# Prompt attention of a hybrid decoder step: the second head's division moved to GpSimd

## The reference, cut to what matters

```python
s = q @ k.T / 8 + bias + log(count)     # 1024 x 1024, causal
e = exp(s - max(s));  p = e / sum(e)
att = p @ v                              # 1024 x 64 for each head
merged = concat(rms_norm(att, g_out_att), rms_norm(y_conv, g_out_conv))
h = h + merged @ w_out
```

## Time and profile before

| | us |
|---|---|
| median of 3 runs | 1403.39 (1402.79 to 1406.4) |
| profiled execution, its own time | 1402.83 |
| its span, first to last instruction | 1401.0 |
| first score matmul of the stage (L1697) starts | 402.1 |
| last matmul of P V (L1724) starts | 551.6 |

### The profile page before, as it was taken

One profiled execution on the slowest core, in us unless ns is written; L12 is line 12 of the kernel. 1 busy time (PEld: TensorE's weight loads), 2 busy tenths in 40 slices (PEclk: granted clock), 3 DMA queues, 4 the chain that ended last, 5 costly groups with the idle time before them and its releaser, 6 DMA issues.

```text
span 1401.0 us, 13600 instructions
## 1 busy us (share of the span) xinstructions
PE 1215.4 (87%) x4994; PEld 651.9 (47%) x4994; DVE 431.5 (31%) x972; ACT 326.2 (23%) x637; POOL 169.5 (12%) x171
## 2 busy tenths in 40 slices
PE   4999999999978887866999938888889898789995
PEld 1444445666645555732455524444344434334442
DVE  1121212221147777311255581411111111033332
ACT  2132322000027664411011110111111111133332
POOL 0001000000030113000001131121212221000000
PEclk9999999999979998877999958999999999979998
DMA  8011400111050102879612054788888888522200
GB/s 271 36 45 60 124 15 19 45 41 64 0 159 31 31 2 62 236 217 325 247 61 72 37 199 140 274 302 354 299 340 300 340 306 344 223 93 98 92 29 34
DMA packets 63660, 209.15 MB, mean 149 GB/s; under 512 B 15198, under 2 KB 28926, under 8 KB 47728
## 3 DMA queue, kind: packets, MB, share of 16 engines
q1 hardware_dynamic: 50560, 177.64, 36.3%
q0 software_dynamic: 13040, 30.71, 5.7%
HBM read 191.81 MB, written 27.52 MB: 157 GB/s over the span
## 4 chain that ended last, share of the span: by engine, by line
PE 71%; DMA 12%; DVE 8%; issue 4%; ACT 3%; POOL 1%; SPq 1%; POOLq 0%; DVEq 0%; ACTq 0%
PE pair L1618 12%; PE pair L1670 12%; PE pair L1939 9%; PE pair L1855 8%; PE pair L2042 8%; DMA R<-m_dram,lists 7%; PE pair L1962 4%; DMA R<-in_cache_v 3%; PE pair L1697 3%; PE pair L1711 2%; PE pair L2024 2%; PE pair L1724 2%; DVE R L1455 2%; DVE R L1229 1%; PE pair L1748 1%
## 5 line engine op out<-in xcount | busy, mean ns | idle before, releaser
L1939 PE MATMUL pair<-R 128*128 128x512 f32 (+1 forms) x512 | 201.3, 617 | 19.9 <-DVE R L1455 19.9
L1670 PE MATMUL pair<-R 128*128 128x352 f32 x576 | 172.5, 463 | 0.4 <-ACT kts L868 0.4
L1618 PE MATMUL pair<-R 128*128 128x512 f32 x384 | 170.2, 601 | 0.8 <-DVE R L1121 0.8
L1670 PEld LDWEIGHTS pair<-R 128*128 128x128 f32 x576 | 110.2, 192 | 61.8 <-issue 1.5
L1939 PEld LDWEIGHTS pair<-R 128*128 128x128 f32 (+1 forms) x512 | 79.6, 180 | 124.8 <-issue 99.1
L1855 PE MATMUL pair<-R 128*128 128x512 f32 x256 | 115.5, 606 | 0.0
L2042 PE MATMUL pair<-R 128*128 128x512 f32 x256 | 114.2, 605 | 0.8 <-ACT R L1053 0.8
L1618 PEld LDWEIGHTS pair<-R 128*128 128x128 f32 x384 | 72.9, 193 | 87.5 <-issue 86.3
L1962 PE MATMUL pair<-R,bias_s 128*128 128x512 f32 (+1 forms) x256 | 98.0, 597 | 0.7 <-ACT bias_s L1009 0.7
L2042 PEld LDWEIGHTS pair<-R 128*128 128x128 f32 x256 | 49.7, 194 | 63.7 <-issue 63.7
L1460 DVE TENSOR_TENSOR R<-pair,R 128x256 f32<-128x256 f32 x27 | 11.5, 425 | 206.6 <-ACT R L1005 206.5
(11 more groups left out here) (280 smaller groups left out, 1280.9 us busy)
## 6 DMA issues: line engine op xcount, KB each, us to landing
R<-in_w_gate SPq DMA_DIRECT2D x32, 1024.0 KB, 8.3
R<-in_w_up SPq DMA_DIRECT2D x32, 1024.0 KB, 11.1
R<-in_w_down SPq DMA_DIRECT2D x32, 1024.0 KB, 5.0
R<-in_x_prompt SPq DMA_DIRECT2D x16, 512.0 KB, 3.4
R<-in_cache_k SPq DMA_DIRECT2D x8, 1024.0 KB, 9.1
R<-in_cache_v SPq DMA_DIRECT2D x8, 1024.0 KB, 18.6
R<-y_dram SPq DMA_DIRECT2D x16, 512.0 KB, 4.3
R<-in_w_in SPq DMA_DIRECT2D x3, 2048.0 KB, 14.9
```

Of the source, the lines that this page charges most:

```text
L1618: last = mm(bk[4 + part][0:n, :], xTs[a.u][:, c, 0:n], wA[:, c, AD * part:AD * part + AD], start=(c == 0), stop=(c == DC - 1))
L1670: last = mm(bk[b][:, 0:n], wB[q % 2][:, c, which, :], xT[:, c, lo:lo + n], start=(c == 0), stop=(c == DC - 1))
L1939: last = mm(bk[2 + u][r, :].rearrange("p (w f) -> p w f", w=2), xgT[u][:, c, r], wgu[s][:, :, c, :], start=(c == 0), stop=(c == DC - 1))
```

## The change

The second head's product moves from DVE's list to Pool's; DVE keeps its reciprocal. `p_ready` becomes two semaphores, one for each head. The squares, the addition and the gain of a pair move from one block behind the pair to single operations behind Pool's division of three successive steps: the squares of pair 0, 1 and 2 stand behind steps 11, 19 and 27, the addition (pairs 1 and 2) behind steps 20 and 28, the gain behind steps 13, 21 and 29. Those of the last pair stand at the end, as before. No other list changes.

```diff
-        for pair in range(NG):
+        def normalise(n, hh):
+            w = P * (STEPS[n][1] + 1)
+            k = 2 * (n % 2) + hh
+            pool.wait_ge(S("rden"), 2 * n + hh + 1)
+            pool.tensor_scalar(E[n % 2][hh][:, 0:w], E[n % 2][hh][:, 0:w], rden[:, k:k + 1], None, ALU.mult).then_inc(S("p_ready1"), 1)
+
+        def squares(pair):
             pool.wait_ge(S("ot_free"), 8 * (pair + 1))
             rows = aT[:, pair, 0:SEQ]
-            if pair >= 1:
-                pool.wait_ge(S("a_sum"), pair)
             if pair == 0:
                 pool.tensor_tensor(a_sum, rows, rows, ALU.mult).then_inc(S("a_sum"), 1)
             else:
                 pool.tensor_tensor(a_sq, rows, rows, ALU.mult).then_inc(S("a_sq"), 1)
...
+        for n in range(NSTEP):
+            normalise(n, 1)
+            pair, k = (n - 3) // 8 - 1, (n - 3) % 8
+            if pair >= 0 and k == 0:
+                squares(pair)
+            if pair >= 1 and k == 1:
+                add_squares(pair)
+            if pair >= 0 and k == 2:
+                scale_a(pair)
+        squares(NG - 1)
+        add_squares(NG - 1)
+        scale_a(NG - 1)
...
+        def invert(n, hh):
+            k = 2 * (n % 2) + hh
+            dve.wait_ge(S("exp_done"), 2 * n + hh + 1)
+            dve.reciprocal(rden[:, k:k + 1], den[:, k:k + 1]).then_inc(S("rden"), 1)
...
             normalise(n, 0)
-            normalise(n, 1)
+            invert(n, 1)
...
-                pe.wait_ge(S("p_ready"), 2 * n + hh + 1)
+                pe.wait_ge(S(f"p_ready{hh}"), n + 1)
```

More of the change, by code:

```diff
@@ L706, in _, with add_squares, scale_a @@
                 pool.tensor_tensor(a_sq, rows, rows, ALU.mult).then_inc(S("a_sq"), 1)
-                pool.wait_ge(S("a_sq"), pair)
-                pool.tensor_tensor(a_sum, a_sum, a_sq, ALU.add).then_inc(S("a_sum"), 1)
-                pool.wait_ge(S("a_sum"), pair + 1)
-            pool.tensor_scalar(rows, rows, gatt[:, pair:pair + 1], None, ALU.mult).then_inc(S("a_scaled"), 1)
+        def add_squares(pair):
+            pool.wait_ge(S("a_sum"), pair)
+            pool.wait_ge(S("a_sq"), pair)
+            pool.tensor_tensor(a_sum, a_sum, a_sq, ALU.add).then_inc(S("a_sum"), 1)
+        def scale_a(pair):
+            rows = aT[:, pair, 0:SEQ]
+            pool.wait_ge(S("a_sum"), pair + 1)
+            pool.tensor_scalar(rows, rows, gatt[:, pair:pair + 1], None, ALU.mult).then_inc(S("a_scaled"), 1)
+        for n in range(NSTEP):
[10 more added lines that the diff above has]
+        scale_a(NG - 1)
         def store_m(a):
@@ L1225, in normalise @@
             k = 2 * (n % 2) + hh
-            dve.wait_ge(S("exp_done"), 2 * n + hh + 1)
-            dve.reciprocal(rden[:, k:k + 1], den[:, k:k + 1]).then_inc(S("rden"), 1)
+            invert(n, hh)
             dve.wait_ge(S("rden"), 2 * n + hh + 1)
-            dve.tensor_scalar(E[n % 2][hh][:, 0:w], E[n % 2][hh][:, 0:w], rden[:, k:k + 1], None, ALU.mult).then_inc(S("p_ready"), 1)
+            dve.tensor_scalar(E[n % 2][hh][:, 0:w], E[n % 2][hh][:, 0:w], rden[:, k:k + 1], None, ALU.mult).then_inc(S("p_ready0"), 1)
         def evac_o(n):
```

## The result

The changed kernel took 1432.3 us (median of 4, 1423.5 to 1433.8) against 1404.0 of the kernel before in the same comparison: ratio 1.0187, 95% interval 1.0143 to 1.023. Two later comparisons of the same two kernels gave 1.0165 (1.0135 to 1.0195) and 1.0168 (1.0132 to 1.0204), medians 1425.4 and 1425.0 against 1401.6 and 1403.4. By the ratios the change is 23 to 26 us slower, by the medians 22 to 28. The forecast was 1427.

What follows compares the result with a forecast made beforehand. The stage was taken as bound by a chain round the engines through the second head's wide divisions. 27.6 + 1.6 - 3.6 + 1.0 - 7.6 + 1.6 + 3.4 = 24.0 on 1402.8 gave 1427 us, range 1413 to 1440.

Steps and rivals of the forecast that it cites:

- the loop: Chain round the engines through the second head's division of even, wide steps; its added cost lengthens the stage one for one.
- Pool's excess: Second head's division in four even steps, 9.50 us on Pool against 2.61 on DVE: plus 27.6 over four pairs.
- hand-over: Extra waits between DVE, Pool and PE around the division: 0.1 us for each even step, plus 1.6.
- slack: Time PE's second-head transposes already wait beyond the division: 0.9 of 1.4 us a pair gained, minus 3.6.
- last step: Step 31's division of 512 counts too, 1.54 us on Pool against 0.49 on DVE: plus 1.0.
- gain product: Pool's 2.88 us product between divisions of steps 13 and 14 and their like delays the wide one 0.5: plus 1.6.
- divisions blocked before: DVE divisions held beside Pool's block at steps 10, 18 and 26 would be freed: minus 7.6 us.
- their two spells: TensorE at its lower clock level behind the long waits of steps 18 and 26 would go: minus 3.4 us.
- spells of the changed kernel: TensorE's lower clock behind PE's waits for Pool, one a pair at 1.7 us, two more than before: net plus 3.4.
- the rival at 17%: The clock falls twice a pair, behind the 1024 and 896 steps: 6.6 to 10 us more, 1435 us; 17%.
- The narrow steps: Odd steps' second-head divisions on Pool run inside the wide steps' chain and cost nothing, except the final one.
- The rival that DVE would be held behind Pool's divisions: First head's divisions wait behind Pool's throughout and the narrow steps' chain becomes the longer one: 1432 us; 14%.

Runs made afterwards that it cites:

- filled kernel: The changed kernel plus identity matmuls on PE ahead of its wait for Pool in even steps, against the kernel before: 1420.5 us, again 1423.8 us (ratio 1.0131).
- spread kernel: Both heads divided on DVE, only Pool's squares, addition and gain product spread over narrow steps, against the kernel before: 1390.2 us, ratio 0.9927.
- wide-only kernel: The changed kernel with Pool dividing the second head only in even, wide steps, narrow ones back on DVE: 1424.9 us, ratio 1.0168 to the kernel before.
- copying one: The changed kernel with Pool copying the second head in place of dividing it: 1388.8 us, ratio 0.9898 to the kernel before.

## Why the prediction was right

It was right in sign and in the mechanism of the loop, and the time lies within its range: 1427 against medians of 1432, 1425 and 1425, or plus 24.0 against 23 to 26 by the ratios. That the number came so near is in part luck: the loop's own cost was put too high and the clock's too low, and the two errors partly cancel. By its own steps:

| step | predicted | measured |
|---|---|---|
| Pool's excess, hand-over, slack, last step, gain product | 27.6 + 1.6 - 3.6 + 1.0 + 1.6 = 28.2 | about 26, an estimate: four periods of 38.5 less 32.3, and 1.0 for the last step. Filled against spread, 169.2 - 138.6 = 30.6, with some 5 for the fill itself |
| divisions blocked before, and their two spells | -7.6 - 3.4 = -11.0 | 138.6 - 149.5 = -10.9 |
| spells of the changed kernel | 6.8 | about 8, 11 and 18 (what is left of the sum below; 3.5, 6.5 and 13.2 against the filled kernel) |
| sum | 24.0 | stage + 23.2, + 26.2, + 32.9 (third, second and first profile) |

*Pool's division.* Predicted 2.88, 2.54, 2.21, 1.87, 1.54 for 1024 to 512; measured 2.84, 2.52, 2.20, 1.88, 1.56. The four wide ones make 9.45 against 9.50.

*The loop.* Shown by the wide-only kernel, which keeps the whole loss, and by the copying one, which loses it.

*The hand-over.* Taken at 0.1 a step. At step 10 the reciprocal ends at 466.97 and Pool starts at 467.06; it ends at 469.58 and PE starts at 469.64. That is 0.15, less about 0.09 for the two waits that it replaces (0.04 from reciprocal to division on DVE, 0.05 from DVE to PE): some 0.06 in place of 0.1.

*Slack* is a term that was mis-sized. In the spread kernel PE's second transposes start 0.36, 0.36 and 0.87 us behind the divisions of 896, 768 and 640, 1.6 a pair; in the changed kernel's three profiles they start 0.05 or 0.06 behind Pool's in every even step but one. All of the slack is used up, and the prediction counted 0.9 of 1.4. The *last step* wasn't measured by itself.

*The gain product.* Predicted a delay of 0.5 in each of three steps. In the first profile there is none at step 14 (the reciprocal ends at 488.16, Pool divides at 488.26), 0.5 at step 22 and 0.4 at step 30: 0.9 in place of 1.6. The second and third profiles have 0.4 at step 14 too, and 1.4 in all; in the first the step before ran longer, with the clock down from 482 to 486, and the product was over in time.

*The blocked divisions and the spreading.* The best term of the sum: -11.0 against -10.9, by the spread-only kernel, and in its parts too (7.6 and 3.4, measured 7.8 and 3.2). What the prediction didn't say is that this half of the change, alone, is faster than the kernel before and than the whole change.

*The clock* is the other term that was mis-sized. One spell a pair was taken. In all three profiles of the change every pair from the second on has two, behind 1024 and behind 896, which is the rival at 17%; its 1435 lies above the medians in part because the loop itself cost less. The executions differ in how long the spells are, and in the first profile there is a third one in the second pair, behind step 12. In the third profile a spell costs 1.4 us behind 1024 (11.71 against 10.27 at full clock) and 1.1 behind 896 (9.8 against 8.74), where 1.7 was taken for each; in the first profile the clock costs up to 4.9 a pair.

*The narrow steps* were counted at nothing but the last. That is right for the change and wrong in general: 6.6 us when the wide ones are short.

From the scores of step 12 to those of step 20 it was 44.1 us (471.95 to 516.09), outside the 39 to 42 that were looked for, again by the clock; in the third profile it was 40.9 (466.62 to 507.56). The rival that DVE would be held behind Pool's divisions did not come: its divisions beside them were extended by 0.37 us at 256 columns, by up to 0.12 at 384 and by nothing at 128. Beside the addition of step 20 one of 384 columns took 2.46 us in place of 0.42; the stretch between the divisions of steps 20 and 22 is 0.15 us longer than that of steps 12 and 14, where no addition stands (8.63 against 8.48, third profile). So the blocked work left on DVE cost next to nothing, as predicted.

## What to carry to other kernels

Ask first whether an engine is busy or only late: here no engine was full, and moving work to the idlest one lengthened the one chain that counts by the difference of two durations. Price a moved operation on the engine that receives it, at each width, and look at where it stands in the other engines' lists. When a change has two parts, run each alone: the half that only looked like preparation was worth 11 us, and the other half threw away 35 (1425.4 against 1390.2, the same comparison). A longer wait of PE can cost twice, once as itself and once in the clock of the work behind it. And work put into a wait to hold the clock up has to be shorter than what is left of the wait, or it becomes the bound; check where the next real instruction starts.

## What the runs showed of the hardware

Pool's tensor_scalar with a pointer scalar goes by 0.28 us and 2.5 ns a column (0.60 at 128, 2.84 at 1024), against 0.22 us and 0.52 ns on DVE (0.29 and 0.75) and 0.19 us and 0.83 ns for Pool's copy.

How Pool's work holds a DVE division depends on the operation and the moment. Beside the squares and the addition DVE was held to Pool's end whenever it began in their first 1.2 us. Beside a tensor_scalar of 1024 columns it was not. In the changed kernel, timeline (the first row lies in the middle of Pool's division of 498.23 to 501.08, shown above):

```profile
499.81 0.29 DVE L1256 TENSOR_SCALAR R<-R,small 128x128 f32<-128x128 f32 x1
...
528.79 2.85 POOL L720 TENSOR_SCALAR R<-R,gatt 128x1024 f32<-128x1024 f32 x1
...
529.81 0.55 DVE L1256 TENSOR_SCALAR R<-R,small 128x640 f32<-128x640 f32 x1
```

Divisions that began 1.0 to 1.6 us into it ran at their usual length, and Pool's did not grow. Of those that began 1.8 us or later, each of 640 or 1024 columns ended 0.34 to 0.55 us behind Pool's end, so they had been held to it. And those that began in its first 0.6 us were held for a while, not to its end. In the wide-only kernel two of 384 columns, begun 0.22 and 0.45 us into it, took 1.10 and 0.88 us in place of 0.42. In the kernel before the one at 455.91 took 1.35 us in place of 0.69, beside this product, which went on to 458.5:

```profile
455.30 3.21 POOL L710 TENSOR_SCALAR R<-R,gatt 128x1024 f32<-128x1024 f32 x1
```

It looks as if a tensor_scalar held what DVE needs in a first and a last part with a gap between them. No run was made to settle it. One case seems to speak against it, in every kernel here but the wide-only one: a division of 1024 columns begun 1.46 us into a product of 1056 columns takes 2.04 us in place of 0.75 and ends 0.55 behind it. At its usual length it would have gone on to 2.2 us into the product, past the 1.8 from which others were held, so it may fit after all.
